# The gates' sigmoid in an MLA stage: exponential on ScalarE, plus one and reciprocal on VectorE

## The reference

```python
a_ret = (ro * silu(rg)) @ w_br
mo = causal_block_attention(q, k, v)          # 8 heads, q and k of width 192, v of width 128
a_mla = mo @ w_bm
mixed = sigmoid(gr) * a_ret + sigmoid(gm) * a_mla      # gr, gm: (h @ w_in) columns, 512 x 1024 each
x = x + mixed @ w_o
```

## Time and profile before

| | |
|---|---|
| three runs | 2001.25, 2001.08, 1999.48 us |
| median | 2001.08 us |
| span of the profiled execution | 1999.3 us, mean granted TensorE clock 0.999 |
| busy | PE 98%, DVE 52%, ACT 40% of the span |

### The profile page before, as it was taken

The page is one execution under the profiler, slowest core; times in us unless marked ns, Lnnn a source line. Parts: engine busy times, 40 slices in busy tenths (PEclk is TensorE's granted clock), DMA queues, the critical chain, the costliest instruction groups (busy, mean ns, idle before and its releaser), DMA issues.

```text
span 1999.3 us, 24017 instructions
## 1 busy us (share of the span) xinstructions
PE 1967.7 (98%) x9144; PEld 1594.7 (80%) x9144; DVE 1044.6 (52%) x1663; ACT 793.5 (40%) x1335; POOL 115.0 (6%) x138
## 2 busy tenths in 40 slices
PE   7999999999999999999999999999999999999998
PEld 6778777888888888877878787777778888888887
DVE  5687877455433544455353534466653553334354
ACT  5343556534222323333232323577752332322243
POOL 2140000002000000200000000000000200000011
PEclk9999999999999999999999999999999999999999
DMA  9842222123333332322223231211223332323321
GB/s 364 325 169 85 64 65 84 64 85 88 86 94 95 105 99 72 124 85 72 97 63 105 63 105 53 65 55 44 57 93 105 127 106 85 105 85 104 94 95 64
DMA packets 196578, 199.64 MB, mean 100 GB/s; under 512 B 7547, under 2 KB 170448, under 8 KB 194064
## 3 DMA queue, kind: packets, MB, share of 16 engines
q1 hardware_dynamic: 192416, 175.15, 28.2%
q0 software_dynamic: 4080, 23.40, 3.0%
HBM read 194.33 MB, written 4.19 MB: 99 GB/s over the span
## 4 chain that ended last, share of the span: by engine, by line
PE 90%; ACT 4%; DVE 3%; issue 1%; DMA 1%; SPq 0%; DVEq 0%; ACTq 0%
PE bank L761 47%; PE bank L1263 4%; PE bank L1014 4%; PE bank L851 4%; PE bank L837 3%; PE bank L1513 3%; PE bank L726 3%; PE bank L1333 2%; PE bank L1069 2%; PE bank L1241 2%; PE bank L881 1%; PE bank L998 1%; PE bank L964 1%; PE bank L1252 1%; PE bank L1283 1%
## 5 line engine op out<-in xcount | busy, mean ns | idle before, releaser
L1629 ACT ACTIVATE w_hi<-raw 128x2048 fp32r<-128x2048 f32 (+4 forms) x165 | 285.1, 1729 | 434.3 <-PE bank L761 306.6
L2372 DVE TENSOR_TENSOR w_lo<-raw,w_hi 128x2048 fp32r<-128x2048 f32 (+4 forms) x163 | 336.8, 2066 | 146.9 <-ACT w_hi L1629 145.0
L761 PE MATMUL bank<-h_hi,w_hi 128*128 128x512 f32 x864 | 337.7, 391 | 0.0
L761 PE MATMUL bank<-h_hi,w_lo 128*128 128x512 f32 x864 | 336.4, 389 | 0.0
L761 PE MATMUL bank<-h_lo,w_hi 128*128 128x512 f32 x864 | 336.1, 389 | 0.0
L761 PEld LDWEIGHTS bank<-h_lo,w_hi 128*128 128x128 f32 x864 | 162.2, 188 | 34.3 <-issue 0.5
L761 PEld LDWEIGHTS bank<-h_hi,w_lo 128*128 128x128 f32 x864 | 162.2, 188 | 34.0
L761 PEld LDWEIGHTS bank<-h_hi,w_hi 128*128 128x128 f32 x864 | 162.2, 188 | 34.0 <-issue 0.5
L761 PE MATMUL bank<-u_hi,w_hi 128*128 128x512 f32 x256 | 100.9, 394 | 0.0
L761 PE MATMUL bank<-u_hi,w_lo 128*128 128x512 f32 x256 | 100.4, 392 | 0.0
L761 PE MATMUL bank<-u_lo,w_hi 128*128 128x512 f32 x256 | 99.4, 388 | 0.0
(11 more groups left out here) (562 smaller groups left out, 4057.1 us busy)
## 6 DMA issues: line engine op xcount, KB each, us to landing
raw<-in_w_in SPq DMA_DIRECT2D x49, 1024.0 KB
raw<-in_w_ff SPq DMA_DIRECT2D x44, 512.0 KB
raw<-in_w_up SPq DMA_DIRECT2D x16, 1024.0 KB
raw<-in_w_down SPq DMA_DIRECT2D x16, 1024.0 KB
raw<-in_w_o SPq DMA_DIRECT2D x8, 1024.0 KB
raw<-in_w_br SPq DMA_DIRECT2D x8, 1024.0 KB
raw<-in_w_in SPq DMA_DIRECT2D x13, 512.0 KB
raw<-in_w_ff SPq DMA_DIRECT2D x8, 768.0 KB
```

The lines of the kernel that those rows point to most:

```text
L761: last = nc.tensor.matmul(dst, a, b, start=k == n == 0, stop=k == last_k and n == 2)
L1629: nc.scalar.activation(w_hi[:, slot, 0:width], raw[:, slot, 0:width], ACT.Copy).then_inc(hi_done, 1)
L2372: v.tensor_tensor(w_lo[:, slot, 0:width], raw[:, slot, 0:width], w_hi[:, slot, 0:width].bitcast(F32), ALU.subtract).then_inc(lo_done, 1)
```

## The change

The activation function of a gate becomes an exponential of the negated input; DVE then adds one in place, takes the reciprocal in place, and multiplies as before. Both new DVE steps are waited for. `exp_table(8)` moves ahead of gate (0, 0), and `exp_table(2 * i)` behind the gates of each pair is left out. `exp_table(2 * i + 1)` behind the roots stays, and so do the sigmoids of the other stages.

```diff
                 def sigmoid(j, m):
                     act.wait_ge(sem("gr_used"), max(2 * j + m - 1, 0))
                     act.wait_ge(mm_done, u_mla(("ga", "gb")[m], j) + 1)
-                    nc.scalar.activation(nt[:, 4 + m, :], bank[2 + m][:], ACT.Sigmoid).then_inc(sem("gr_out"), 1)
+                    nc.scalar.activation(nt[:, 4 + m, :], bank[2 + m][:], ACT.Exp, scale=-1.0).then_inc(sem("gr_out"), 1)
...
                 split(u_mla("ga", 1))
+                exp_table(8)
                 sigmoid(0, 0)
-                exp_table(8)
...
                             sigmoid(i, 1)
                             if i < 3:
                                 sigmoid(i + 1, 0)
-                            exp_table(2 * i)
...
                 def gated(j, m):
                     dve.wait_ge(sem("gr_out"), 2 * j + m + 1)
+                    own.step(v.tensor_scalar(nt[:, 4 + m, :], nt[:, 4 + m, :], 1.0, None, ALU.add))
+                    own.step(v.reciprocal(nt[:, 4 + m, :], nt[:, 4 + m, :]))
                     v.tensor_tensor(aret[:, 2 * j + m, :], aret[:, 2 * j + m, :], nt[:, 4 + m, :], ALU.mult).then_inc(sem("gr_used"), 1)
```

## The result

| | before | changed |
|---|---|---|
| median | 2000.99 us (4 runs, 1999.48 to 2001.25) | 2035.38 us (4 runs, 2033.01 to 2036.23) |
| span of the profiled execution | 1999.3 us | 2033.0 us |
| mean granted TensorE clock | 0.999 | 0.991 |

The ratio is 1.0172, 95% interval 1.0159 to 1.0185: the change makes the kernel 34.4 us slower. The forecast was 2033.9. The times of the kernel before fall in two groups, near 1999.4 and near 2001.0 us, so a difference of two medians can be off by some 1.6 us, as the first experiment shows.

What follows compares the result with a forecast made beforehand. PE, busy 98% of the span, was taken as the bound, with DVE releasing it in the MLA stage. Stops net of loads, 28.0 us, plus 4.8 of slow clock made 32.8 over the median 2001.08: 2033.9 us, range 2022 to 2042.

Steps and rivals of the forecast that it cites:

- The bound and the place: MLA stage, step 2 of pairs: gates stand ahead of `values` and `peak`, so DVE's added work stops PE.
- The rival in which DVE's idle time takes the work: MLA stage: 57 us idle on DVE absorb the 31 added, only the loads' 3.3 us count: 1997.8 us; 3 in 100.
- The prices: Eight gates on DVE: add 0.49 us, reciprocal 3347 ns, waits 0.03 us each; 3.9 us per gate, 31.2 us in all.
- The 0.14 us read as slack: Pair 1: `values` ends at 1368.28, PE's third key/value projection waiting for that copy starts at 1368.42.
- What the loads give back: Nine table loads go, 11.5 us of ACT; 3.3 us return on the path, in pairs 0 to 3.
- gate (0, 0), to turn 1: Gate ahead of the first peak: 3.9 us of DVE plus 0.1 for `exp_table(8)`'s activation, 4.0 us.
- pair 0, turn 1 to 3: Two gates at step 2 of pair 0: 7.8 - 1.33 = 6.5 us, plus 1.6 us of slow clock.
- pair 1, turn 10 to 11: Two gates at step 2 of pair 1: 7.8 - 0.25 = 7.55 us, plus 1.6 us of slow clock.
- pair 2, turn 18 to 19: Two gates at step 2 of pair 2: 7.8 - 0.25 = 7.55 us, plus 1.6 us of slow clock.
- pair 3, turn 24 to 28: One gate at step 2 of pair 3: 3.9 - 1.5 = 2.4 us.
- The clock: Behind the three long PE stops: a stretch at 1.2 GHz costs 1.6 us each, 4.8 us in all.
- the full-clock case: Rival for the MLA stage: full PE stops without a clock fall, + 28 us, 2029 us; 22 in 100.

Runs made afterwards that it cites:

- the first experiment: The changed kernel without the add and the reciprocal on DVE, ScalarE's half alone: 1997.50 us, ratio 0.9988 to the kernel before.
- the spread kernels: The changed kernel with all gates' reciprocals but the first's in quarters over a pair's steps: 2012.14 us; the same without quarters in step 7: 2004.56 us.
- the slope of one: From the changed kernel with each reciprocal done twice, 27.0 us more on DVE: 2064.01 us, 28.6 us over the changed kernel.
- the spread kernel: The changed kernel with the reciprocals of all gates but the first in quarters of 128 columns over a pair's steps, step 7 included: 2012.14 us, ratio 1.0057.
- the filled kernel: The changed kernel with 28 unread matmuls in PE's queue at step 3 of pairs 0 to 2, ahead of the waiting projection: 2030.93 us, ratio 1.0151.
- the kernel with the first gate left: The changed kernel with add and reciprocal left out at gate (0, 0) alone: 2029.90 us, ratio 1.0149 to the kernel before.

## Why the prediction was right

- **The bound and the place.** That DVE's free 57 us aren't free room, since `values` and `peak` stand behind the gates and PE asks at once, was the step on which the sign hung. The stops of 7.2 us, the level shift between the gates, the spread kernels and the slope of one bear it out. The rival in which DVE's idle time takes the work would need the spread kernel's schedule; it isn't the one of the change.
- **The prices.** Reciprocal 3353 ns (3347 taken), add 421 ns (0.49 us taken, too much by 0.07). A gate adds 0.46 + 3.38 = 3.84 us by the timeline, 3.9 were taken. The 0.14 us read as slack are hardly any: in the changed kernel, where PE does wait for the copy, it starts 0.15 us behind its end.
- **What the loads give back.** 3.3 us were forecast: 1.33 in pair 0, 0.25 in each of pairs 1 and 2, 1.5 in pair 3. Behind DVE's added work they are worth 0.27 and 0.27 in pairs 1 and 2 and 1.45 in pair 3, as forecast. In pair 0 about 1.5 are left over once DVE's work and the clock are taken off the growth of the shift; no run gives this number alone. Without the added work the same loads give 1.12, 0.04, 0.04 and 1.05, and the forecast for that kernel was too high by 1.3 us.
- **The five terms.** The measured column is the growth of the shift, from turn to turn; the stage itself starts 0.27 us earlier in the changed kernel, and `exp_table(8)` adds 0.2 to the first. The clock's part is that of the filled kernel in pairs 0 to 2, elsewhere what the turns behind the stop take over those of before (5.44 against 4.26, 6.24 against 4.76):

| place | forecast | measured | DVE's work | loads | clock |
|---|---|---|---|---|---|
| gate (0, 0), to turn 1 | 4.0 | 4.98 + 0.27 = 5.25 | 3.84 + 0.2 | | 1.2 |
| pair 0, turn 1 to 3 | 8.1 | 12.33 - 4.98 = 7.35 | 7.68 | -1.5 (the rest) | 1.2 |
| pair 1, turn 10 to 11 | 9.15 | 21.68 - 12.17 = 9.51 | 7.68 | -0.27 | 2.0 |
| pair 2, turn 18 to 19 | 9.15 | 29.97 - 21.47 = 8.50 | 7.68 | -0.27 | 1.0 |
| pair 3, turn 24 to 28 | 2.4 | 33.67 - 29.79 = 3.88 | 3.84 | -1.45 | 1.5 |

- **The clock.** Its fall was forecast at the three long stops at 1.6 us each, 4.8 in all; the filled kernel gives 4.2. So the size was right, but not because every rest brings one such stretch: it was 1.0 to 2.0 us at equal rests, and in the spread kernel 1.6 or nothing. The mis-sized step is that nothing was taken in the sum for the stop at step 0 and for the last pair. The clock fell at both, and they took 1.2 and 1.5 us more. These 2.7 us are more than the difference between 32.8 and the measured 34.4; against them DVE's work came out 0.5 us under the 31.2 and the three long stops 0.6 under the 4.8, so the closeness of the sum is in part luck. No run filled the two other stops, but the kernel with the first gate left has neither the stop at step 0 nor the longer turn. The fall goes with the earlier trace rows and with the warning of the Trainium skill ("TensorE: Matmul & The Clock Gate", section "Why this matters for your kernels") against rests of PE between bursts, with which the trace agrees at the stops of 3.77 and 7.2 us.
- **The range.** Its lower end is told as four fifths of the full-clock case, which is 22.4 us over the kernel before and thus 2023.5, not 2022. Nothing hangs on it.
- **One step was told wrongly, at no cost.** I had PE stop at the turn of step 0, behind DVE. It stops one instruction earlier, at a turn of keys that waits for a copy by ACT (L2152), which itself stands behind the exponential of step 0 and so behind DVE. The stop was put at 3.3 us and is 3.77.
- **The drain at a load.** The Trainium skill, "ScalarE: Activation LUTs", section "What ACT_TABLE_LOAD costs", adds a drain of 1.38 us to a load. The trace differs: the activation starts 1.30 us after its load does, and ahead of all the loads of one line together ACT stood idle only 0.1 us.

## What to carry to other kernels

Read a new instruction's price against the slack of the place where it stands in its engine's queue, not against that engine's share of the span: 31 us of work on a half-idle VectorE cost 38 us in one place, and 27 of them, in quarters between steps that wait anyway, about 2. A function switch on ScalarE is worth what the next engine leaves of it (here 2.0 of 11.5 us alone, about 3.5 together with VectorE's work); before trading it for work elsewhere, look for an identity within the table that is in use, as tanh for the sigmoid. Where a change makes TensorE stand for microseconds, add the half-rate work that follows, at every such stop, here 1.0 to 2.0 us each. And where a kernel's times fall in groups, compare group with group before a small gain is read from medians.

## What the runs showed of the hardware

- The reciprocal over 128x512 takes 3.35 us on VectorE, 8 times the add of the same shape (0.42) and nearly 5 times a product (0.69).
- A fused (tensor plus scalar) times tensor took 684 ns at 128x512, as the plain product did (686).
- Tanh and the exponential need no table load between them; a sigmoid and the exponential do (1283 ns each way).
- The clock behind a rest wasn't the same each time. Behind PE's rest near 20 us it stayed at 1.00 in three profiled executions (rests of 1.25, 1.39 and 1.58 us) and fell to 0.50 in seven (1.87 to 2.90 us). In the spread kernel it stayed behind one rest of 2.42 us and fell behind two of 2.43. A fall there costs 1.6 us, and the one near 20 us makes the two groups of a kernel's times, as far as the ten profiles tell.
- The clock fell not only in rests of 7 us. In the last pair PE rested 1.63 and 1.36 us with 0.7 us of work between, and was granted half the clock behind them (PE's timeline and windows of the changed kernel):

```profile
1490.93 0.68 PE L1416 MATMUL bank<-nt,vv 128*128 128x128 f32 x4 [1.63 <-DVE mo_lo L3148]
1492.97 0.69 PE L1409 MATMUL bank<-ident,nt 128*128 128x128 f32 x2 [1.36 <-DVE nt L3143]
```
```profile
1492.00:1494.00 2.00, 1.03 (x3) 0.82 (x4) 1.37 (x4) 1.32 (x5) 0.00 (x0) 0.64 0.98 317
1494.00:1496.00 2.00, 2.00 (x5) 1.01 (x4) 0.00 (x0) 0.08 (x1) 0.00 (x0) 0.51 0.50 175
1496.00:1498.00 2.00, 2.00 (x10) 1.65 (x9) 1.02 (x3) 0.68 (x3) 0.00 (x0) 1.00 0.00 0
```
